# The softmax factors of 24 attention units multiplied on GpSimd instead of VectorE

## The reference

```python
# sliding window, 8 query heads on 2 key heads, window 128, with a sink
p = jnp.exp(s - m)
p = p / (jnp.sum(p, axis=-1, keepdims=True) + jnp.exp(sink - m))
# cross attention to 256 memory tokens, 4 heads of 256 channels (in both layers)
p = jax.nn.softmax(s, axis=-1)
# sparse attention, 4 groups of 4 heads, selected and window branch
ps = jax.nn.softmax(ss...); o_s = einsum(ps, vg)
pw = jax.nn.softmax(...);   o_w = einsum(pw, vwb)
return gb[..., 0:1] * o_c + gb[..., 1:2] * o_s + gb[..., 2:3] * o_w
```

## Time and profile before

| | |
|---|---|
| median of 3 runs | 2634.9 us (2632.81 to 2636.02) |
| the profiled execution | 2630.73 us |
| its span, first to last instruction | 2628.8 us |
| mean granted TensorE clock | 0.983 |
| TensorE busy | 2491.2 us (95%) |
| VectorE busy | 1940.7 us (74%) |
| ScalarE busy | 1296.4 us (49%) |
| GpSimd busy | 0.2 us, 4 instructions |

### The profile page before, as it was taken

How to read it: one execution, slowest core, us unless ns; L and a number is a source line. 1 busy time by engine, 2 the same in 40 slices (tenths; PEclk the granted TensorE clock), 3 DMA queues, 4 the chain that set the end, 5 groups by cost and what they waited for, 6 DMA issues and landing times.

```text
span 2628.8 us, 44531 instructions
## 1 busy us (share of the span) xinstructions
PE 2491.2 (95%) x18672; PEld 2367.2 (90%) x18672; DVE 1940.7 (74%) x2383; ACT 1296.4 (49%) x1414; POOL 0.2 (0%) x4
## 2 busy tenths in 40 slices
PE   7799899999998999799998889999999999999998
PEld 6689899998998999799997679999999999999996
DVE  5555587868565897854555658888888888888887
ACT  3443433344423333233321527767676767676764
POOL 0000000000000000000000000000000000000000
PEclk9999999999999999999998999999999999999999
DMA  5124245542341445344531029999989999899995
GB/s 217 65 86 155 75 151 185 184 153 97 121 145 65 160 178 179 137 177 177 177 126 36 1 67 363 341 340 345 339 344 342 341 342 343 339 343 341 342 342 212
DMA packets 77091, 556.77 MB, mean 212 GB/s; under 512 B 8544, under 2 KB 8672, under 8 KB 9952
## 3 DMA queue, kind: packets, MB, share of 16 engines
q1 hardware_dynamic: 75888, 547.45, 56.4%
q10 hardware_dynamic: 1008, 6.49, 0.7%
HBM read 552.86 MB, written 1.05 MB: 211 GB/s over the span
## 4 chain that ended last, share of the span: by engine, by line
PE 87%; DVE 7%; ACT 3%; issue 2%; DMA 1%; SPq 0%; DVEq 0%; ACTq 0%
PE ps L749 13%; PE ps L751 13%; PE ps L750 13%; PE ps L1237 12%; PE ps L1239 12%; PE ps L1238 12%; PE ps L841 2%; PE ps L812 2%; PE ps L1231 1%; PE ps L1277 1%; PE ps L866 1%; PE ps L756 1%; PE ps L1051 1%; DVE wlo L1363 1%; ACT whi L466 1%
## 5 line engine op out<-in xcount | busy, mean ns | idle before, releaser
L1363 DVE TENSOR_TENSOR wlo<-raw,whi 128x2048 fp32r<-128x2048 f32 x519 | 1185.0, 2288 | 266.6 <-ACT whi L466 208.0
L466 ACT ACTIVATE whi<-raw 128x2048 fp32r<-128x2048 f32 x519 | 994.1, 1916 | 638.0 <-PE ps L751 483.9
L749 PE MATMUL ps<-hh,whi 128*128 128x256 f32 x2336 | 670.2, 287 | 33.3 <-DVE hl L1431 28.9
L750 PE MATMUL ps<-hl,whi 128*128 128x256 f32 x2336 | 663.2, 284 | 0.0
L751 PE MATMUL ps<-hh,wlo 128*128 128x256 f32 x2336 | 663.0, 284 | 0.0
L1237 PE MATMUL ps<-whi,hh 128*128 128x256 f32 x1792 | 523.4, 292 | 3.6 <-DVE work L2010 3.6
L1239 PE MATMUL ps<-wlo,hh 128*128 128x256 f32 x1792 | 507.8, 283 | 0.0
L1238 PE MATMUL ps<-whi,hl 128*128 128x256 f32 x1792 | 507.6, 283 | 0.0
L749 PEld LDWEIGHTS ps<-hh,whi 128*128 128x128 f32 x2336 | 450.6, 193 | 40.2 <-DVE hl L1431 34.4
L750 PEld LDWEIGHTS ps<-hl,whi 128*128 128x128 f32 x2336 | 450.8, 193 | 0.3
L751 PEld LDWEIGHTS ps<-hh,wlo 128*128 128x128 f32 x2336 | 450.5, 193 | 0.0
(11 more groups left out here) (314 smaller groups left out, 2690.1 us busy)
## 6 DMA issues: line engine op xcount, KB each, us to landing
raw<-stream SPq DMA_DIRECT2D x519, 1024.0 KB, 4.8
work<-w_in ACTq DMA_DIRECT2D x1, 2240.0 KB, 9.5
stage<-stage_consts ACTq DMA_DIRECT2D x4, 512.0 KB, 4.7
work<-mem_in ACTq DMA_DIRECT2D x2, 1024.0 KB, 4.8
x<-x_in SPq DMA_DIRECT2D x1, 1024.0 KB, 5.0
out<-x SPq DMA_DIRECT2D x4, 256.0 KB, 2.3
const<-consts SPq DMA_DIRECT2D x1, 548.5 KB, 5.9
par<-params SPq DMA_DIRECT2D x1, 405.5 KB, 6.5
```

The lines of the kernel that those rows point to most:

```text
L466: nc.scalar.activation(whi[hi_at(g, odd)][:, :], raw[g % RAWS][:, :], ACT.Copy).then_inc(hi_ready, 1)
L749: mm(out_ap, hi_w, hi_x, start=start, stop=False, **kw)
L750: mm(out_ap, hi_w, lo_x, start=False, stop=False, **kw)
L1363: V.tensor_tensor(wlo[g % RAWS][:, :], raw[g % RAWS][:, :], whi[hi_at(g, odd)][:, :].bitcast(F32), ALU.subtract).then_inc(lo_ready[g % RAW ...
```

## The change

VectorE no longer multiplies the probabilities. It computes the factors and signals `factors_ready`, and it no longer waits for the last small operation itself. GpSimd gets a program of its own for all 24 units: it waits for the factors of a unit, does its four multiplies and signals `probs_ready`. Order, buffers and waits of the other engines stay. Ahead of the expert stage GpSimd waits for the flag as before.

```diff
--- before.py
+++ after.py
@@ -227,6 +227,7 @@
         negmax_ready = sem("negmax_ready")
         exp_done = sem("exp_done")
         probs_ready = sem("probs_ready")
+        factors_ready = sem("factors_ready")
         pt_ready = sem("pt_ready")
         pt_copied = sem("pt_copied")
         pv_done = sem("pv_done")
@@ -438,6 +439,21 @@
                 nc.gpsimd.tensor_tensor(wlo[g % RAWS][:, :], raw[g % RAWS][:, :], whi[hi_at(g, odd)][:, :].bitcast(F32),
                                         ALU.subtract).then_inc(lo_ready[g % RAWS], 1)
 
+            def scale_probs(kind, u0):
+
+                for step, (g, qt, br) in enumerate(units(kind)):
+                    u = u0 + step
+                    pr, s0, nk = PROBS[u % 3], STATS[u % 3], P * key_tiles(kind, qt)
+                    pool.wait_ge(factors_ready, u + 1)
+                    for h in range(4):
+                        ins = nc.gpsimd.tensor_scalar(pr[:, h * 256:h * 256 + nk], pr[:, h * 256:h * 256 + nk],
+                                                      small[:, s0 + 16 + h:s0 + 17 + h], None, ALU.mult)
+                    ins.then_inc(probs_ready, 1)
+
+            scale_probs("swa", SWA_U)
+            scale_probs("xa", XA_U[0])
+            scale_probs("xa", XA_U[1])
+            scale_probs("nsa", NSA_U)
             with pool.If(few_flag(pool)):
                 pass
             with pool.Else():
@@ -1508,16 +1524,15 @@
                         dve.wait_ge(exp_done, u + 1)
                         if kind == "swa":
                             link(V.tensor_tensor(small[:, s0 + 4:s0 + 8], small[:, s0 + 4:s0 + 8], small[:, s0 + 12:s0 + 16], ALU.add))
-                        link(V.reciprocal(small[:, s0 + 16:s0 + 20], small[:, s0 + 4:s0 + 8]))
+                        recip = V.reciprocal(small[:, s0 + 16:s0 + 20], small[:, s0 + 4:s0 + 8])
                         if kind == "nsa":
+                            link(recip)
                             at = 64 + qt * 48 + g * 12
                             coef = small[:, s0 + 16:s0 + 20].rearrange("p (par j) -> p par j", par=2)
-                            link(V.tensor_tensor(coef, coef, small[:, at:at + 12].rearrange(
-                                "p (j par b) -> p par j b", j=2, par=2)[:, :, :, br + 1], ALU.mult))
-                        for h in range(4):
-                            ins = V.tensor_scalar(pr[:, h * 256:h * 256 + nk], pr[:, h * 256:h * 256 + nk],
-                                                  small[:, s0 + 16 + h:s0 + 17 + h], None, ALU.mult)
-                        ins.then_inc(probs_ready, 1)
+                            V.tensor_tensor(coef, coef, small[:, at:at + 12].rearrange(
+                                "p (j par b) -> p par j b", j=2, par=2)[:, :, :, br + 1], ALU.mult).then_inc(factors_ready, 1)
+                        else:
+                            recip.then_inc(factors_ready, 1)
                     if st >= 3:
                         u = u0 + st - 3
                         g, qt, br = us[st - 3]
```

## The result

The changed kernel takes 2652.8 us (median of 4 runs, 2652.51 to 2652.99), the kernel before 2635.5 us beside it (4 runs, 2632.81 to 2637.66): a ratio of 1.0067 [1.0052, 1.0082], or +17.4 us. The prediction was +4.9 us, with a range to 2650. The profiled execution took 2652.7 us, its span is 2650.9.

What follows compares the result with a forecast made beforehand. TensorE was taken to bound the kernel (95% busy, 87% of the chain), mostly weight streaming. Terms +1.7 + 0 - 0.2 + 0.5 + 2.9 = +4.9 us on 2634.9 gave 2639.8 us, range 2634 to 2650.

Steps and rivals of the forecast that it cites:

- price of an instruction: Each GpSimd multiply: 0.47 us for 256 columns, 0.36 us for 128, taken from ScalarE's rows.
- The ends of 0.29 and 0.69: Bounds per 256-column GpSimd multiply: VectorE's own 0.29 us, a two-operand VectorE operation's 0.69; far end 1.23.
- rival 2: Sparse attention's cover is gone, t above 0.525 us; at 0.69 the kernel takes +12.6 us, 2647.5; chance 0.42.
- Handoffs, 0.2 us for both: Each moved block: signals VectorE to GpSimd and GpSimd to TensorE cost 0.2 us together.
- Cross attentions, +0.86 us to the first transposes: First block of each cross attention: 1.22 us becomes 2.08 on the path; +1.7 us for two.
- The second block is not added again: Cross attentions: second transposes wait for the first unit's copy, which moves by the same 0.86 us; no extra cost.
- TensorE's clock, +2.9 us in the first cross attention: First cross attention: longer idle makes the granted clock fall there too, +2.9 us; already lost in the second.
- Sparse attention, nothing: Sparse attention's 16 units: a 2.08 us block fits the 2.3 us cover, costing nothing up to t = 0.525 us.
- 8 x (4t - 2.1): Sparse attention past its cover: each of 8 wide units adds 4t - 2.1 us, t being the price per instruction.
- Sliding window, +0.5 us: Sliding window attention: first transposes, masks and all behind move some 0.5 us; ends 0.0 and +1.1.
- VectorE's freedom, -0.2 us: Sparse attention: in four places the block delays evacuation and next maximum; removing it gains 0.2 us for all four.
- Rival 3: GpSimd and VectorE hinder each other, an instruction nears 1.23 us, a narrow one 0.94: +50 us, 2685; chance 0.06.

Runs made afterwards that it cites:

- one-instruction kernel: The changed kernel with GpSimd multiplying each whole unit in a single TENSOR_TENSOR, factors broadcast along the keys: 2635.8 us, 1.0003 against the kernel before.
- kernel with filled gaps: The changed kernel with 36 more zero products ahead of the first and 16 ahead of the second transposes of each cross attention: 2651.2 us, 1.0063.
- two heads: The changed kernel with GpSimd multiplying two heads of each unit and VectorE the other two, TensorE waiting for both: 2634.4 us, 1.0004.
- control: The kernel before, word for word, run once more for its scatter and a second profile: 2634.4 us, 0.9999.
- kernel with the constant: The changed kernel with GpSimd multiplying by a constant 0.25 instead of each row's factor: 2646.2 us, 1.0045 against the kernel before.

## Why the prediction was wrong

The step that failed is the price of an instruction. A second step, that the second block of a cross attention adds nothing, failed with it. Forecast and measured growths, by attention: sliding window 0.5 and 3.8 us, first cross attention 3.8 (with the clock) and 5.6, second 0.9 and 3.4, sparse 0 and 9.2.

**The price of an instruction: the term that was mis-sized.** "I take 0.47 us, a plain pass of one engine over 256 columns" and 0.36 us for 128. Measured: 0.905 and 0.585 us. The ends of 0.29 and 0.69 did not hold it; only the far end of 1.23 did, and that had 0.06. I had taken ScalarE's row as the price of a plain pass over the same columns. The argument against rival 2, that it needs an engine slower than ScalarE, was no evidence: no row had GpSimd's arithmetic. That the first use of an operation might be dear is not it either, as all 14 wide blocks last the same. The one-instruction kernel shows that the error is in this form on this engine, not in GpSimd's arithmetic as such: two inputs cost 1.67 ns a column, one input and a factor 2.5. The estimate that stood beside the prediction, 0.38 us by halving a figure of the Trainium skill (GPSIMD Engine Reference, "Elementwise — side-by-side cycle accounting"), is farther off still.

**Handoffs, 0.2 us for both:** right, 0.15 to 0.21.

**Cross attentions, +0.86 us to the first transposes:** by its own formula with the measured price, 4 x 0.905 + 0.2 - 1.22 = 2.6 us; measured 3.77 - 1.22 = 2.55. The formula held.

**"The second block is not added again":** this failed in its own right. The argument was that copy and second block move by the same amount. That is true of when the second block could start, not of when GpSimd is free for it. The second factors are final 2.1 us behind the first (299.50 + 0.18 against 297.58); a block longer than that queues. Price: 3.60 - 2.30 = +1.3 us in each cross attention. At the assumed price the step was just true: in the one-instruction kernel, with 1.89 us, the second transposes start 2.30 us behind the first. So it should have been given its own threshold, and I had given one to the sparse attention only.

**TensorE's clock, +2.9 us in the first cross attention:** the fall came, at 302; the second transposes took 1.97 against 1.06 us, and the kernel with filled gaps puts its price at 1.7 us. Direction right, size 1.2 us high. The spell at 0.50 is no shorter than the one that I had priced it from: here the windows from 302 to 308 have 0.50 and the next 0.84, there those from 834 to 840 have 0.50 and the next 0.86. But here TensorE stood idle for 2.03 us of it, waiting for the second block. Where the block had the assumed length the clock cost 2.7 us (two heads) and 1.6 (one instruction). With these terms the first cross attention is 2.55 + 1.3 + 1.7 = 5.6 us, its measured growth. The second, which had lost its clock already, is 3.9; measured 3.4 against the profile of before and 4.7 against the control's.

**Sparse attention, nothing:** the mechanism was right, its threshold too as far as the kernels bracket it, and the price put the change on its far side. Rival 2 is what happened, beyond its own 0.69 us. "8 x (4t - 2.1)" gives 12 us at t = 0.905 and 9.2 was measured. It takes each wide unit for itself, but they come in pairs. The first of a pair pays 3.77 - 2.32 = 1.45 us. The second queues behind it in GpSimd, as in the cross attentions: its transposes start 3.60 us behind the first ones where it was 3.26, so it pays 0.34. And the narrow units whose cover is 2.32 us do not stay hidden: 4 x 0.585 + 0.15 = 2.49 us is past it by 0.17. From pair to pair, four units, the attention goes from 15.2 to 17.0 us at full clock. That the clock falls inside the sparse attention was in none of my cases: the four units in which it does so (from 1464.6 to 1482.4) take 17.8 us, 0.8 more than the next four. The last pair, with a gap of 2.85 us ahead of it where it was 1.60, loses the clock as well. That these 0.8 us are the clock's is read from one profile. The kernel with the constant, whose blocks are 3.29 instead of 3.62 us and whose narrow ones fit the cover again, keeps its clock from 1462 up to the last pair and takes 16.3 us for each four units.

**Sliding window, +0.5 us:** measured +3.8. At the measured price the first transposes move by 1.55 us instead of 0.7, and the masks behind them by 1.1 instead of 0.5. The clock, which in before stays at 1.00 until 110, falls at 104: these masks and their scores take 1.60 and 2.08 us instead of 1.21 and 1.13, which is 1.3 more. The last wide block, 3.61 us, no longer fits its cover and adds the other 1.4.

**VectorE's freedom, -0.2 us:** nothing larger was seen. In the sparse attention two heads on GpSimd relieve VectorE of half its block at no cost in waits, and it takes 65.6 us as before.

**Rival 3** had the engines blocking each other, from a rule of the Trainium skill (SBUF — State Buffer, "Who interferes with whom"): a whole instruction locked out. Whether VectorE's multiply runs in such a mode no trace here shows. In the kernel with two heads both multiply at once: GpSimd's pair takes 1.98 us instead of 1.82, VectorE's 0.84 instead of 0.62. They slow each other by 9% and 36%, and neither waits for a whole instruction of the other: VectorE's second one begins and ends while GpSimd's first (1.08 us, 0.92 otherwise) is running. In the changed kernel VectorE's small operation took up to 0.42 us beside a block (0.17 otherwise), 0.5 us over all 24. And GpSimd's wide blocks last 3.61 to 3.62 us whatever VectorE does beside them. So it is no part of the 17 us that could be told.

## What to carry to other kernels

Ask of a moved block two things: does it still fit the cover between its input and its consumer, and does the next block come in before the engine is through with this one? Each gives a price per instruction at which the answer turns, and if the price is not in the trace, the chances belong on both sides of that number; here it was 0.525 us and my guess lay 10% under it. A block whose time is known on one engine has no known time on another: one kernel with a single such instruction would have given the price. On GpSimd, a multiply by a column of factors was better written as one TENSOR_TENSOR with the factor repeated than as four TENSOR_SCALARs (1.89 against 3.62 us). Even so it only matched VectorE here: the 23 us that VectorE gave up bought nothing that can be told.

## What the runs showed of the hardware

- GpSimd's TENSOR_SCALAR on f32 cost 2.5 ns a column and 0.29 us (0.21 with a constant), 0.905 us for 256 columns in a block of four, three times VectorE's 0.29. TENSOR_TENSOR cost 1.67 ns a column and 0.19 us, although it has a second tensor operand.
- VectorE and GpSimd multiplying in SBUF at once slowed each other by a part (36% and 9%), and VectorE lost more.
- The granted clock fell to 0.50 behind gaps of TensorE that had grown: from 1.83 to 4.37 us (first cross attention), from 0.51 to 1.68 (sparse, 1468.70) and from 1.71 to 3.22 (sliding window). It did not fall where zero products left 0.60 us of such a gap. The length of one gap alone does not decide: it held behind 1.53 us twice in the sparse attention, and before the change the same gap of 1.83 us kept it in the first cross attention and lost it in the second.
